# Fewer staged and more split blocks of weights, and a last turn that finishes one token half before the other

## What is computed

```python
for layer in range(DEPTH):                     # DEPTH = 2
    if layer == 0: y = _rglru_mixer(x, ...)    # x @ w_in, conv, gates, scan, @ w_out
    else:          y = _moba_mixer(x, ...)     # x @ w_qkv, softmax, @ w_out
    x = _layer_norm(DEEPNORM_ALPHA * x + y, ln_g[layer, 0], ln_b[layer, 0])
    h = jax.nn.relu(x @ mlp_w1[layer])
    x = _layer_norm(DEEPNORM_ALPHA * x + (h * h) @ mlp_w2[layer],
                    ln_g[layer, 1], ln_b[layer, 1])
```

## Time and profile before

| | us |
|---|---|
| median of 3 runs | 2142.0 |
| lowest and highest run | 2140.47, 2144.07 |
| the profiled execution's own time | 2144.91 |
| its span, first to last instruction | 2143.1 |
| TensorE busy | 2122.6 |
| VectorE busy | 1306.1 |
| ScalarE busy | 973.7 |
| GpSimd busy | 29.8 |
| mean granted TensorE clock | 0.998 |

### The profile page before, as it was taken

One profiled execution on the slowest core, in us unless ns is written; L12 is line 12 of the kernel. 1 busy time (PEld: TensorE's weight loads), 2 busy tenths in 40 slices (PEclk: granted clock), 3 DMA queues, 4 the chain that ended last, 5 costly groups with the idle time before them and its releaser, 6 DMA issues.

```text
span 2143.1 us, 30984 instructions
## 1 busy us (share of the span) xinstructions
PE 2122.6 (99%) x10948; PEld 1807.5 (84%) x10948; DVE 1306.1 (61%) x1240; ACT 973.7 (45%) x1085; POOL 29.8 (1%) x22
## 2 busy tenths in 40 slices
PE   9999999999999999999999999999999999999997
PEld 8898888888888888888888888888888888888886
DVE  6769665665645554565766666676655545645556
ACT  5595444434434443443544445344434434434442
POOL 0000010000000000000100000010000000000000
PEclk9999999999999999999999999999999999999999
DMA  8666666666566666656555556665666566566664
GB/s 278 190 186 198 222 207 182 190 191 191 179 198 184 194 188 195 186 187 187 167 165 168 164 165 220 196 200 181 195 193 187 186 196 186 177 202 181 194 192 133
DMA packets 210481, 406.13 MB, mean 190 GB/s; under 512 B 12480, under 2 KB 18880, under 8 KB 209376
## 3 DMA queue, kind: packets, MB, share of 16 engines
q1 hardware_dynamic: 210112, 402.90, 60.5%
q10 hardware_dynamic: 288, 2.10, 0.3%
HBM read 402.85 MB, written 2.10 MB: 189 GB/s over the span
## 4 chain that ended last, share of the span: by engine, by line
PE 97%; DVE 1%; issue 1%; ACT 0%; DMA 0%; SPq 0%; DVEq 0%; ACTq 0%
PE ps L368 40%; PE ps L358 34%; PE ps L359 17%; PE ps L591 1%; PE ps L589 1%; PE ps L590 1%; PE ps L499 0%; PE ps L604 0%; PE ps L472 0%; PE ps L471 0%; PE ps L470 0%; PE ps L579 0%; DVE bnst L1047 0%; DVE f L1040 0%; DMA f<-in_x_dram 0%
## 5 line engine op out<-in xcount | busy, mean ns | idle before, releaser
L840 DVE TENSOR_TENSOR wl<-wst,wh 128x1024 fp32r<-128x1024 f32 x744 | 903.1, 1223 | 665.2 <-ACT wh L622 663.2
L622 ACT ACTIVATE wh<-wst 128x1024 fp32r<-128x1024 f32 x744 | 783.0, 1059 | 909.6 <-PE ps L368 469.4
L358 PE MATMUL ps<-xin,wh 128*128 128x512 f32 x3072 | 1088.6, 399 | 1.8 <-issue 1.3
L359 PE MATMUL ps<-xin,wl 128*128 128x256 f32 x3072 | 862.6, 281 | 0.0
L358 PEld LDWEIGHTS ps<-xin,wh 128*128 128x128 f32 x3072 | 577.3, 188 | 145.0 <-issue 1.7
L368 PE MATMUL ps<-wh,hid 128*128 128x512 f32 x2560 | 694.9, 389 | 0.0
L359 PEld LDWEIGHTS ps<-xin,wl 128*128 128x128 f32 x3072 | 580.4, 189 | 0.2
L368 PEld LDWEIGHTS ps<-wh,hid 128*128 128x128 f32 x2560 | 479.9, 188 | 99.4
L368 PE MATMUL ps<-wl,hid 128*128 128x512 f32 x1280 | 404.5, 389 | 0.0
L368 PEld LDWEIGHTS ps<-wl,hid 128*128 128x128 f32 x1280 | 240.3, 188 | 50.0
L850 DVE TENSOR_TENSOR e<-e,ps 128x1024 f32<-128x1024 f32 x32 | 39.1, 1221 | 50.2 <-ACT e L631 50.2
(11 more groups left out here) (114 smaller groups left out, 651.2 us busy)
## 6 DMA issues: line engine op xcount, KB each, us to landing
wst<-in_mlp_w_dram SPq DMA_DIRECT2D x512, 512.0 KB, 3.8
wst<-in_moba_w_qkv_dram SPq DMA_DIRECT2D x96, 512.0 KB, 4.3
wst<-in_rg_w_in_dram SPq DMA_DIRECT2D x64, 512.0 KB, 4.4
wst<-in_rg_w_out_dram SPq DMA_DIRECT2D x32, 512.0 KB, 4.8
wst<-in_moba_w_out_dram SPq DMA_DIRECT2D x32, 512.0 KB, 4.6
gate<-in_ln_g_dram SPq DMA_DIRECT2D x3, 1024.0 KB, 8.1
gate<-in_ln_b_dram SPq DMA_DIRECT2D x3, 1024.0 KB, 10.1
f<-in_x_dram SPq DMA_DIRECT2D x8, 256.0 KB, 8.2
```

The costliest lines, as they stand in the source:

```text
L358: pe.matmul(dst[:, n, :], wh[:, s, w], src[:, c, :, :], start=(c == 0), stop=False)
L359: mm = pe.matmul(dst[:, n, 0:T], wl[:, s, w], src[:, c, 0, :], start=False, stop=(c == NC - 1))
L622: act.activation(wh[:, off % SPLITS, :], wst[:, kb, :], ACT.Copy).then_inc(wh_done, 1)
L840: dve.tensor_tensor(wl[:, off % SPLITS, :], wst[:, off % BLOCKS, :], wh[:, off % SPLITS, :], ALU.subtract).then_inc(wl_done, 1)
```

## The change

The stage has 4 slots instead of 8 and the splits 8 instead of 4, so both together still hold 12 blocks. AHEAD becomes 7, so START, LATE and NEXT become 9, 14 and 17. The load of a block now waits for the split of the block four earlier, a split for TensorE's use of the block eight earlier; at the start, the fifth to eighth load wait too. The last turn does its first token half over all eight blocks, then the second. Its splits are dealt out anew: the turn before it splits all of its blocks (up to NEXT - 1 = 16), none is left within the first half, and between the two halves' adds stand more. The extra room comes from `e1` and `e2`, which move into `f2`, and from a smaller scratch for DMA descriptors. In the diff `last_pair` is ScalarE's, the pieces after it VectorE's `last_turn`.

```diff
+STAGE = 4
-SPLITS = 4
-AHEAD = 4
+SPLITS = 8
+AHEAD = 7
-HELD = BLOCKS - SPLITS
-        e1 = sb("e1", [P, GROUP, T])
-        e2 = sb("e2", [P, GROUP, T])
-        wst = sb("wst", [P, BLOCKS, BLK])
+        wst = sb("wst", [P, STAGE, BLK])
+        e1 = f2[:, 0:1024].rearrange("p (c t) -> p c t", t=T)
+        e2 = f2[:, 1024:2048].rearrange("p (c t) -> p c t", t=T)
...
             def load_block(src, kb, b):
+                slot = kb % STAGE
                 if b is not None:
-                    sp.wait_ge(wl_done, b - (BLOCKS - 1))
-                sp.dma_start(wst[:, kb, :].rearrange("p (k n) -> p k n", k=KCH), src)\
-                  .then_inc(stage_full[kb], 16)
+                    sp.wait_ge(wl_done, b - (STAGE - 1))
+                sp.dma_start(wst[:, slot, :].rearrange("p (k n) -> p k n", k=KCH), src)\
+                  .then_inc(stage_full[slot], 16)
...
-                load_block(first[kb], kb, None)
+                load_block(first[kb], kb, None if kb < STAGE else kb)
...
             def last_token_turn(b, ready):
-                for kb in range(HELD):
-                    pe.wait_ge(pair_ready, ready + (kb + 1))
-                    pe.wait_ge(wl_done, b + kb + 1)
-                    for c in range(kb * KCH, (kb + 1) * KCH):
-                        for a in range(HALVES):
-                            for part, low in ((0, 0), (0, 1), (1, 0)):
-                                mm = token_step(1, a, c, part, low)
-                    mm.then_inc(mm_done, 1)
                 for a in range(HALVES):
-                    for kb in range(HELD, BLOCKS):
+                    for kb in range(BLOCKS):
...
              def last_pair(b, no, n):
-                splits(b, no, START, NEXT)
+                splits(b, no, START, NEXT - 1)
                 b, no = b + BLOCKS, no + 1
-                splits(b, no, START, BLOCKS)
...
                 if n < 3:
-                    splits(b, no, BLOCKS, BLOCKS + 3)
+                    splits(b, no, BLOCKS, BLOCKS + 7)
...
-                    if k in (1, 2, 3):
-                        off = BLOCKS + 2 + k
+                    if k in (3, 5):
+                        off = BLOCKS + 7 + (k - 3) // 2
                         splits(b, no, off, off + 1)
...
-                splits(b, START, BLOCKS)
                 add_half(0)
...
                 inverse(0)
-                splits(b, BLOCKS, BLOCKS + 2)
+                splits(b, BLOCKS, BLOCKS + 6)
                 add_half(1)
...
                     split_norm(k)
-                    if k < 4:
-                        off = BLOCKS + 2 + k
+                    if k in (3, 5, 7):
+                        off = BLOCKS + 6 + (k - 3) // 2
                         splits(b, off, off + 1)
...
-    nc = _bacc.Bacc("TRN2", target_bir_lowering=False, num_devices=1)
+    nc = _bacc.Bacc("TRN2", target_bir_lowering=False, num_devices=1, dynamic_dma_scratch_size=8192)
```

More of the change, by code:

```diff
@@ L140, in build_trunk @@
         std, rstd = tok[:, 0, :], tok[:, 1, :]
-        stage_full = [sem(f"stage_full{s}") for s in range(BLOCKS)]
+        stage_full = [sem(f"stage_full{s}") for s in range(STAGE)]
         x_loaded = [sem(f"x_loaded{k}") for k in range(BLOCKS)]
@@ L258, in _ @@
                 n0 = (gb // 4) * 4 + (gb % 2) * 2
-                sp.wait_ge(wl_done, B_GATES + gb - (BLOCKS - 1))
-                sp.dma_start(wst[:, gb, :].rearrange("p (k n) -> p k n", n=LRU_W),
+                sp.wait_ge(wl_done, B_GATES + gb - (STAGE - 1))
+                sp.dma_start(wst[:, gb % STAGE, :].rearrange("p (k n) -> p k n", n=LRU_W),
                              w[0, n0:n0 + 2].rearrange("n (k p) v -> p (n k) v", p=P))\
-                  .then_inc(stage_full[gb], 16)
+                  .then_inc(stage_full[gb % STAGE], 16)
             with sp.Fori(0, NG) as t:
@@ L616, in split_hi @@
             def split_hi(b, turn_no, off):
-                kb = off % BLOCKS
-                act.wait_ge(stage_full[kb], turn_no * 16 + 16 * (off // BLOCKS + 1))
+                slot = off % STAGE
+                act.wait_ge(stage_full[slot], turn_no * (16 * BLOCKS // STAGE) + 16 * (off // STAGE + 1))
                 if not (isinstance(b, int) and b + off < SPLITS):
                     act.wait_ge(mm_done, b + (off - (SPLITS - 1)))
-                act.activation(wh[:, off % SPLITS, :], wst[:, kb, :], ACT.Copy).then_inc(wh_done, 1)
+                act.activation(wh[:, off % SPLITS, :], wst[:, slot, :], ACT.Copy).then_inc(wh_done, 1)
             def splits(b, turn_no, lo=AHEAD, hi=AHEAD + BLOCKS):
@@ L665, in _ @@
                     conv_hi_part(t - 1)
-                splits(b, t, AHEAD + CONV, LATE)
+                splits(b, t, AHEAD + CONV if t else BLOCKS, LATE)
                 take_hl(t % 2, b, u3[:, t * GROUP:(t + 1) * GROUP, :], hl_copied)
@@ L839, in split_lo @@
                     dve.wait_ge(mm_done, b + (off - (SPLITS - 1)))
-                dve.tensor_tensor(wl[:, off % SPLITS, :], wst[:, off % BLOCKS, :], wh[:, off % SPLITS, :],
+                dve.tensor_tensor(wl[:, off % SPLITS, :], wst[:, off % STAGE, :], wh[:, off % SPLITS, :],
                                   ALU.subtract).then_inc(wl_done, 1)
@@ L1107, in out_unit @@
                     if t == NG - 1:
+                        dve.wait_ge(prepped, NG * n + t + 1)
                         last_turn(b, free + t, n)
@@ L1112, in out_unit @@
                     add_turn(t % 2, b, cols_for(t))
-                    splits(b, LATE, NEXT)
+                    splits(b, LATE, NEXT if t < NG - 2 else NEXT - 1)
                     statistics(t, free + t + 1)
```

## The result

The changed kernel is slower: 2149.3 us median of 10 runs against 2142.5, a ratio of 1.0029 with a 95% interval of 1.0020 to 1.0039. The forecast was 2144.0 (range 2139.0 to 2148.0), "no change that can be told" with 0.83. The loss is past the bound of 0.2% and past the range.

A forecast was written before the change was run, and what follows sets the result against it. TensorE's matmuls were taken to bound the kernel, so only the places where they stop count. 3 x (1.55 - 0.3) - 1.8 = +1.95 us on 2142.0 gave 2144.0 us, range 2139.0 to 2148.0.

The forecast's parts named there:

- What bounds the kernel: Whole kernel: TensorE, busy 99% of the span, never waits for weights; buffers can only matter where the matmuls stop.
- The end, -1.8: Kernel's end, n = 3: the second half's add starts right at the last matmul's end, a gain of 1.8 us.
- The late load: Three inner places: the sixth block's weights land late and delay the second add, +1.55 us at each.
- The bound of 4.6: Inner places: if the sixth block's load takes 4.6 us, the second add is delayed by 1.65 us.
- rival 2: Inner places: the burst of four loads slows all of them; slower, 2149.4 us at a 6.3 us load; chance 0.12.
- VectorE's scalings, -0.3 at each: Inner places: GpSimd's scalings end before VectorE's, which take about 0.41 us each; a gain of 0.3 us per place.
- The clock: Inner places: TensorE's 2.3 us standstill could lower its granted clock; up to +9.8 us, chance 0.04, zero in the sum.
- Nothing elsewhere: Plain turns, row loads and kernel start: no added cost; the closest cover, at the start, is 1.5 us.
- Rival 3: Inner places: TensorE's clock falls for one block's length, 3.25 us at each; up to +9.8, 2153.8 us; chance 0.04.

The follow-up runs named there:

- warm: The changed kernel with eight more warm-up matmuls right behind the last turn's last matmul at n = 0 to 2; 2144.4 us.
- five: The changed kernel with five splits instead of six on VectorE before the second add, six instead of seven on ScalarE; 2142.2 us.
- four: The changed kernel with four splits instead of six on VectorE before the second add, five instead of seven on ScalarE; 2140.2 us.
- oldturn: The changed kernel's four stage and eight split slots, but the last turn in the order of the kernel before; 2142.9 us.
- endonly: The run oldturn with the new order of the last turn at n = 3 alone, the kernel's end; 2142.4 us.

## Why the prediction was wrong

**What bounds the kernel: right.** Every difference that the change made, as far as the runs show, lies where the matmuls stop.

**The end, -1.8: right**, to 0.05 us in the trace.

**The late load: right in place and mechanism, somewhat short in size.** The step put the landing of the sixth block's load at 4.5 us and the delay at 1.55; landings of 4.4, 5.3 and 4.7 made 1.5, 2.3 and 1.7, 5.5 us against 4.65. The bound of 4.6 came from three pairs of loads; in the new burst two more were issued behind the second, at A + 6.7 and at 7.9 to 8.4. In the nine places of the changed kernel, warm and five the second load landed after 4.1 to 5.3 us with the same issues ahead of it, the first after 3.6 to 3.9. So at one place of the three, n = 1, the load took the 5.3 us that rival 2 (0.12) had named. Why one burst is slower than another is open. four and five show the term as a whole: without the second load on the path the delay is gone.

**VectorE's scalings, -0.3 at each: nearly right**, -0.4 at n = 0 (6.35 to 5.93, clock full) and in warm. They took 0.54 us each and not the cast's 0.41, and the cast then waited for ScalarE's first pair, as the step had it. GpSimd's second operation took 5.1 us beside the splits (4.0 at n = 1) instead of 2.99, so that GpSimd ended at A + 14.5 at n = 0, later than the 13.4 of the sum but before VectorE's scalings (A + 14.6). At n = 1 one split took 1.62 us instead of 1.22 beside GpSimd, and four did in warm (1.61 to 1.69), a sign of the exclusion that the Trainium skill states (SBUF — State Buffer, Who interferes with whom) on the side where the rows of before had shown none.

**The clock: the step that failed.** The rival was named, with its place and its mechanism, and given 0.04. It failed in two ways. It took the one fall that the trace of before shows, some 3 us after the kernel's last matmul, as a length that a standstill must reach. The fall came 2.1 us after the last matmul at n = 1, and with a standstill of 2.50 us at n = 2, while the 2.27 us of n = 0 passed without one; the estimate of 2.3 us of standstill lay among these, not below them. One interval at the end of a kernel says when the clock fell once, not how much is safe. And its price of a whole block of turns was too high: the fall hits warm-up matmuls and transposes that stand before the turn, and is over soon. It cost 1.8 and 1.3 us in the profile, where the rival had 3.25 at each of three. In numbers: 5.5 - 1.25 + 3.1 = 7.4 us at the inner places (late load, scalings, clock), where the sum had 3.75; 3.1 of the 3.6 us missed are the clock's, a term that the sum put at nothing. Rival 3 as it stood gave 2153.8; the time fell between it and the forecast. Another 0.5 us is the base: the prediction took 2142.0, the median of ten runs is 2142.5.

**Nothing elsewhere: right.** oldturn is at the time of before. The start shows no wait for weights. One small wait of 0.8 us is new, at the gates, for ScalarE's sigmoids behind a table load of 1.28 us; oldturn (0.6) and four (0.7) have it too, warm and five don't.

## What to carry to other kernels

When a change moves work ahead of the step that restarts TensorE, add up how long TensorE will stand still, and whether the clock can fall in it. Here 0.8 us never cost it, 2.27 us passed once, and 2.50, 2.79 (three times) and 3.09 us did not, nor did 2.24 us near the start of endonly. No run shows how much between 0.8 and 2.2 us is safe. Filling the standstill with matmuls that need nothing took 4.8 us off the changed kernel. A deeper queue of finished work bought with a shallower queue of landed work only holds at an even pace; where slots come free twice as fast, as in the second pass here, check each needed item back to the issue of its load. Before the critical add, what was staged ahead of the burst was safe here (four), its first load just so (five, with 0.25 us to spare), its second not.

## What the runs showed of the hardware

The pace of plain turns is not quite constant. In the changed kernel's chain, identical code (four turns with their four sets of transposes) runs from the first to the second line of each pair:

```profile
309.42 0.47 PE ps L359
...
401.75 87.10 PE ps L369 x384
...
1425.81 0.47 PE ps L359
...
1516.70 87.07 PE ps L369 x384
```

That is 92.33 us and then 90.89, both at a full clock and without a wait. The cause isn't known. One such step is as large as most of the effects sought, so each place is better measured from A, its own start, than from the span.
